# Two transformer blocks on one core: context and x share each weight, modulation sums move to TensorE, attention steps spread by one tile

## What is computed

```python
def first_block(x, c, ...):
    for l in range(2):
        sh1, sc1, gt1, sh2, sc2, gt2 = split(silu(c) @ w_ada[l] + b_ada[l], 6)   # modulation: 1024 -> 6144
        h = rms_norm(x) * (1 + sc1) + sh1
        # h @ w_in, latents, softmax attention and stick-breaking attention, gated merge
        x = x + gt1 * (merged @ w_out[l])
        h = rms_norm(x) * (1 + sc2) + sh2
        x = x + gt2 * ((silu(a) * v) @ w_down[l])       # a, v = split(conv3(h @ w_up[l]))
    return x

def second_block(x, c, ctx, c_ctx, ...):
    for i in range(2):
        mod_x, mod_c = silu(c) @ w_mod[i] + b_mod[i], silu(c_ctx) @ w_mod[i] + b_mod[i]
        hx, hc = rmsnorm(x) * (1 + sc_x) + sh_x, rmsnorm(ctx) * (1 + sc_c) + sh_c
        if i == 0:                     # same weights for hx and hc
            yx, yc = conv_module(hx), conv_module(hc)   # 1024->2048, gate, depthwise conv of 31 taps, layernorm, 1024->1024
        else:                          # keys and values of x and of the context, queries of x
            yx = attention(hx, keys(hx, hc), values(hx, hc))
        x = x + g_x * rmsnorm(yx)      # and ctx likewise while i == 0
        x = x + gf_x * rmsnorm((silu(f @ w1) * (f @ w3)) @ w2)    # and ctx likewise while i == 0
    return x
```

## Time and profile before

| | before |
|---|---|
| median of 3 runs | 3748.67 us (3745.18 to 3753.87) |
| profiled execution | 3750.82 us, its span 3749.0 us, mean granted clock 0.968 |
| busy: PE, DVE, ACT, POOL | 91%, 62%, 38%, 30% |
| HBM read | 368.85 MB, 99 GB/s over the span |
| instructions | 41475 |

### The profile page before, as it was taken

One profiled execution on the slowest core, in us unless ns is written; L12 is line 12 of the kernel. 1 busy time (PEld: TensorE's weight loads), 2 busy tenths in 40 slices (PEclk: granted clock), 3 DMA queues, 4 the chain that ended last, 5 costly groups with the idle time before them and its releaser, 6 DMA issues.

```text
span 3749.0 us, 41475 instructions
## 1 busy us (share of the span) xinstructions
PE 3405.9 (91%) x15776; PEld 2677.8 (71%) x15776; DVE 2312.8 (62%) x3179; ACT 1432.3 (38%) x2194; POOL 1132.4 (30%) x867
## 2 busy tenths in 40 slices
PE   5989999999989998999789997599999977799998
PEld 3757778886658777777659975357888656668886
DVE  6764466564857779496967669944233776643233
ACT  3433233333433233232554454354222455542222
POOL 4404545553404544444411005500000126500000
PEclk8999999999999999999889998799999989999999
DMA  6404535543303434444228721112332100013332
GB/s 207 128 14 124 153 125 159 175 144 90 112 6 121 146 116 122 119 118 138 74 71 241 228 78 45 34 45 85 90 101 79 57 29 1 1 57 96 101 92 66
DMA packets 552730, 373.66 MB, mean 100 GB/s; under 512 B 28861, under 2 KB 526871, under 8 KB 551508
## 3 DMA queue, kind: packets, MB, share of 16 engines
q1 hardware_dynamic: 522928, 278.19, 25.6%
q0 software_dynamic: 29408, 92.76, 7.5%
q10 hardware_dynamic: 196, 0.07, 0.0%
HBM read 368.85 MB, written 2.10 MB: 99 GB/s over the span
## 4 chain that ended last, share of the span: by engine, by line
PE 68%; DVE 24%; issue 3%; ACT 3%; DMA 2%; SPq 0%; POOL 0%; DVEq 0%; ACTq 0%
PE PS L397 18%; PE PS L399 18%; PE PS L398 18%; DVE mod_acc L1086 4%; DVE CV L1232 3%; PE PS L445 3%; DVE tmp L1232 2%; PE PS L468 2%; DVE cv L1575 1%; DVE Wl L1042 1%; PE PS L742 1%; DVE stat_t L1107 1%; PE PS L885 1%; DVE small L1613 1%; PE PS L492 1%
## 5 line engine op out<-in xcount | busy, mean ns | idle before, releaser
L397 PE MATMUL PS<-Hh,Wh 128*128 128x512 f32 (+1 forms) x2816 | 1068.8, 380 | 89.0 <-DVE Wl L1042 62.3
L398 PE MATMUL PS<-Hl,Wh 128*128 128x512 f32 (+1 forms) x2816 | 1045.6, 371 | 0.0
L399 PE MATMUL PS<-Hh,Wl 128*128 128x512 f32 (+1 forms) x2816 | 1045.0, 371 | 0.0
L2100 POOL TENSOR_TENSOR Wl<-raw,Wh 128x1024 fp32r<-128x1024 f32 (+2 forms) x254 | 580.2, 2285 | 711.3 <-ACT Wh L1667 709.4
L397 PEld LDWEIGHTS PS<-Hh,Wh 128*128 128x128 f32 x2816 | 540.5, 192 | 212.1 <-issue 123.8
L1667 ACT ACTIVATE Wh<-raw 128x1024 fp32r<-128x1024 f32 (+2 forms) x558 | 541.2, 971 | 323.8 <-PE PS L399 284.5
L1042 DVE TENSOR_TENSOR Wl<-raw,Wh 128x1024 fp32r<-128x1024 f32 (+2 forms) x304 | 351.0, 1155 | 446.7 <-ACT Wh L1667 446.0
L1086 DVE SCALAR_TENSOR_TENSOR mod_acc<-mod_w,cact,mod_acc 128x256 f32<-128x256 f32 (+1 forms) x644 | 549.5, 895 | 98.7 <-DMA mod_w<-in_w_ada 78.9
L398 PEld LDWEIGHTS PS<-Hl,Wh 128*128 128x128 f32 x2816 | 540.8, 192 | 92.4 <-issue 6.8
L399 PEld LDWEIGHTS PS<-Hh,Wl 128*128 128x128 f32 x2816 | 540.2, 192 | 90.0
L397 PE MATMUL PS<-g_h,Wh 128*128 128x512 f32 (+1 forms) x880 | 337.0, 383 | 14.2 <-DVE g_l L1167 12.5
(11 more groups left out here) (305 smaller groups left out, 4499.5 us busy)
## 6 DMA issues: line engine op xcount, KB each, us to landing
raw<-in_ffn_w SPq DMA_DIRECT2D x132, 512.0 KB, 3.8
mod_w<-in_w_mod POOLq DMA_DIRECT2D x192, 256.0 KB, 3.7
raw<-in_w_up SPq DMA_DIRECT2D x88, 512.0 KB, 4.5
mod_w<-in_w_ada POOLq DMA_DIRECT2D x160, 256.0 KB, 4.0
raw<-in_w_in SPq DMA_DIRECT2D x62, 512.0 KB, 4.2
raw<-in_conv_w_pw SPq DMA_DIRECT2D x48, 512.0 KB, 4.0
raw<-in_ffn_w SPq DMA_DIRECT2D x48, 384.0 KB, 3.3
raw<-in_ffn_w SPq DMA_DIRECT2D x48, 320.0 KB, 3.1
```

The source lines that it names most:

```text
L397: pe.matmul(o, wh, xh, start=start, stop=False, skip_group_check=True)
L398: pe.matmul(o, wh, xl, start=False, stop=False, skip_group_check=True)
L399: return pe.matmul(o, wl, xh, start=False, stop=stop, skip_group_check=True)
L2100: pool.tensor_tensor(low, src, high.bitcast(F32), ALU.subtract).then_inc(*mark("w_low_pool", one[0]))
```

## The change

1. The context is no longer a pass of its own. `conv_both`, `ffn_both` and one `attention_inputs` use every split slab for the 512 columns of x and the 256 of the context (`both`: three matmuls on 512 columns, then three on 256, in two neighbouring PSUM banks). The convolution's buffers hold x, 15 zeros and the context side by side (783 columns), so one instruction does a tap for both; of the taps DVE now has 14, PE 8 and ACT with POOL 9. The feed forward goes in groups of four chunks (`F_GROUPS`). In norms x comes first and then the context, with statistics of its own. The context's input is transposed in the last feed forward of block 1, and x's first squares of block 2 are summed in that feed forward's second half.
2. Modulation: DVE's sums and POOL's loads are gone. SP loads 128x2048 values at a time (1 MB) into one `mod_w`, and a unit on PE (`mod_rows`) is four float32 matmuls of 512 columns with the conditioning vector (one or two columns) as the weights, each to another group of 32 partitions of bank 7. After eight units DVE copies the bank to `mod_row` and PE transposes it (`mod_turn`). There are 8 units in the start-up and 88 in block 1, one after every second slab (every third in the first layer's output product and feed forward).
3. Attention: transposes of tile n-4 instead of n-3 in step n, and the product with the values two steps later.

```diff
-    DVE_TAPS, PE_TAPS = 17, 5
+    SPAN = SEQ + PAD + CTX
+    C_AT = SEQ + PAD
+    DVE_TAPS, PE_TAPS = 14, 8
...
+        def both(job, w, i, cols, x, c, first, last, streams="xc"):
+            b, wh, wl = bank_of[job], w[0][:, i, cols], w[1][:, i, cols]
+            for o, src, one in ((PS[:, b, :], x, "x"), (PS[:, b + 1, 0:CTX], c, "c")):
+                if one in streams:
+                    mm = three(o, wh, wl, src[0], src[1], first, last)
+            return mm
...
+        def mod_rows(block_of, r, w):
+            job, b = ("mod", *block_of), block_of[0]
+            if r == 0:
+                begin(job, "mod")
+            for j in range(4):
+                mm = pe.matmul(PS[32 * j:32 * j + b, bank_of[job], :], cact[b][:, r, :], w[:, 512 * j:512 * (j + 1)],
+                               start=r == 0, stop=r == KD - 1, skip_group_check=True)
+            return mm
+
+        def mod_turn(block_of):
+            job = ("mod_t", *block_of)
+            begin(job)
+            pe.wait_ge(*free(("mod", *block_of)))
+            for q in range(4):
+                mm = pe.transpose(bank(job)[:, q * P:(q + 1) * P], mod_row[:, q * P:(q + 1) * P], const("ident"))
...
-                pe.wait_ge(*ready("mod_w_used", last_tile[g]))
-                for v in range(vs):
-                    for j in range(lo // P, (lo + w) // P):
-                        mm = pe.matmul(bank(job)[:, col:col + 1], acc[n % 2][:, c:c + P], const("ones")[:, 0:1],
+                if what == "rows":
+                    pe.wait_ge(*ready("mod_w_in", block_of, r))
+                    mm = mod_rows(block_of, r, mod_w)
...
+        def ffn_both():
+            for lo, hi in F_GROUPS:
+                for f in range(lo, hi):
...
+                        for x in "13":
+                            linear_both(("up" + x, 0, "x", f), w[x], ("f", 0, "c"))
+                for j in range(KD):
...
+                    for f in range(lo, hi):
+                        mm = both(job, w, f - lo, slice(j % 2 * P, (j % 2 + 1) * P), (g[0][0], g[1][0]), (g[0][1], g[1][1]),
+                                  f == lo, f == hi - 1)
...
-            for n in range(len(tiles) + 5):
+            for n in range(len(tiles) + 7):
                 if n < len(tiles):
                     scores(n, *tiles[n])
-                if n >= 6 and n % 2 == 0:
-                    pv((n - 6) // 2)
-                if 0 <= n - 3 < len(tiles):
-                    turn(n - 3, *tiles[n - 3])
+                if n >= 8 and n % 2 == 0:
+                    pv((n - 8) // 2)
+                if 0 <= n - 4 < len(tiles):
+                    turn(n - 4, *tiles[n - 4])
...
-        load_x("c")
         pre(("n", 0, "c"), CTX)
-        conv_module("c")
-        pre(("f", 0, "c"), CTX)
-        ffn_2(0, "c")
-        pre(("n", 1, "c"), CTX)
-        attention_inputs("c")
-        pre(("n", 0, "x"), SEQ)
-        conv_module("x")
-        pre(("f", 0, "x"), SEQ)
-        ffn_2(0, "x")
-        pre(("n", 1, "x"), SEQ)
-        attention_inputs("x")
+        conv_both()
+        for s in ("x", "c"):
+            pre(("f", 0, s), NS[s])
+        ffn_both()
+        for s in ("x", "c"):
+            pre(("n", 1, s), NS[s])
+        attention_inputs()
...
+            while mod_units and n >= (before[2] + 5 if before else 4):
+                block_of, r, _ = unit = mod_units.pop(0)
+                if before:
+                    sp.wait_ge(*(full(("mod", *before[0])) if before[1] == KD - 1 else ready("mod_w_used", *before[0:2])))
+                sp.dma_start(mod_w[:, :], w_mod.rearrange("(p t) c -> p t c", t=KD)[:, r, :])\
+                  .then_inc(*mark("mod_w_in", block_of, r, by=16))
```

More of the change, by code:

```diff
@@ new lines, in conv_both, with diagonal_taps @@
+                norm_stats(("post", ("conv", "x")), j - 1)
+            norm_stats(("post", ("conv", "x")), KD - 1)
+        def diagonal_taps(j):
+            job = ("taps", j)
+            begin(job, "pair")
+            pe.wait_ge(*free(("pw1a", "x", j)))
+            pe.wait_ge(*ready("diag", j, PE_TAPS - 1))
+            o = banks2(job, SPAN)
+            for at_s in (slice(0, SEQ), slice(C_AT, SPAN)):
+                for k in range(PE_TAPS):
+                    tap = DVE_TAPS + k
+                    mm = pe.matmul(o[:, at_s], diag[:, k, :], U[j % 2][:, at_s.start + tap:at_s.stop + tap],
+                                   start=k == 0, stop=k == PE_TAPS - 1)
@@ L1236, in conv_module @@
                 early_sum = tmp_free[i] = own(dve.tensor_tensor(accs[0], accs[0], accs[1], ALU.add))
+                if j + 1 < KD:
+                    gate(j + 1)
             add_late(KD - 1, early_sum)
-            job = ("mean", s)
-            dve.wait_ge(*full(job))
-            for c in range(KD):
-                ins = dve.scalar_tensor_tensor(CV[:, c, 0:n], bank(job, n), -1.0 / D, CV[:, c, 0:n], ALU.mult, ALU.add)
-                ins.then_inc(*(empty(job) if c == KD - 1 else mark("centred", s, c)))
@@ L1254, in conv_module @@
-            for j in range(KD):
-                ahead(("pw2", s, j))
-            post_norm(("conv", s), n, Y, lambda c: col(2, 0, s, 8, c))
+            where = {"x": slice(0, SEQ), "c": slice(C_AT, SPAN)}
+            for s in ("x", "c"):
+                job, n = ("mean", s), NS[s]
+                dve.wait_ge(*full(job))
+                for c in range(KD):
+                    ins = dve.scalar_tensor_tensor(CV[:, c, where[s]], bank(job, n), -1.0 / D, CV[:, c, where[s]],
+                                                   ALU.mult, ALU.add)
+                    ins.then_inc(*(empty(job) if c == KD - 1 else mark("centred", s, c)))
@@ new lines, in conv_both @@
+                for k in range(PE_TAPS):
+                    act.activation(diag[:, k, :], const("ident"), ACT.Identity,
+                                   scale=vec("w_dw", (DVE_TAPS + k) * KD + j)).then_inc(*mark("diag", j, k))
+                act.wait_ge(*free(("pw1a", "x", j)))
+                if j >= 2:
+                    act.wait_ge(*ready("conv", j - 2))
+                for k in range(-1, LATE_SUMS - 1):
+                    if j + 1 < KD and k in (1, 5):
+                        ahead(("pw1a" if k == 1 else "pw1g", "x", j + 1))
@@ new lines, in conv_both @@
+                    act.activation(o[:, :], U[j % 2][:, tap:tap + SPAN], ACT.Identity, scale=vec("w_dw", tap * KD + j))\
+                       .then_inc(*mark("tap_product", j, k))
+            finish(KD - 1)
+            where = {"x": slice(0, SEQ), "c": slice(C_AT, SPAN)}
+            for s in ("x", "c"):
+                for c in range(KD):
+                    act.wait_ge(*(free(("mean", s)) if c == KD - 1 else ready("centred", s, c)))
+                    square((("ln", s), c), CV[:, c, where[s]], NS[s])
+                root(("ss", ("ln", s)), NS[s])
@@ new lines, in conv_both @@
+            ahead(first_slab(("ln", "x")))
+            act.wait_ge(*full(tally.h_before["ln", "x"]) if tally.h_before.get(("ln", "x")) else full(("pw1g", "x", KD - 1)))
+            for s in ("x", "c"):
+                for c in range(KD):
+                    act.wait_ge(*ready("ln_pre", ("ln", s), c))
+                    o = tb((("ln", s), c))[:, 0:NS[s]]
+                    act.wait_ge(*own(silu(o, o, bias=vec("ln_b", c))))
+                    act.activation(h_of(("ln", s))[0][:, c, :], o, ACT.Copy).then_inc(*mark("h_high", ("ln", s), c))
```

871 lines of the change are left out of this document (463 added, 408 removed).

## The result

| | before | changed |
|---|---|---|
| median, 4 runs each | 3751.27 us | 3641.58 us (3640.9 to 3642.1) |
| ratio | | 0.971 (95% interval 0.969 to 0.973) |
| span of the profiled execution | 3749.0 us | 3639.6 us |

The change made the kernel 2.9% faster. I had forecast faster, but by 0.7% (3723 us). The measured time lies inside the range and nearest to rival A (3609).

A forecast was written before the change was run, and what follows sets the result against it. PE was taken as the main bound, DVE in the convolution's loop, waits in attention. From 3749 us, shared pass -98, modulation on TensorE +114 and attention -42 gave 3723 us, 45 either way; the wider range ran from 3575 to 3835.

The forecast's parts named there:

- rival A: Modulation on PE: all four column groups run at once, 1.06 us a unit, 3609 us in all; chance 0.33.
- T = 5 x 0.43 + 0.20 = 2.35: Cost in us of one modulation unit on PE, partly overlapped; 88 units in block 1 add 207 us.
- The bounds 1.06 and 3.64: Modulation unit's cost in us: all four matmuls overlapping, or none; the latter was a rival at 3837 us, chance 0.18.
- The middle case: Modulation unit: records start in program order, so only neighbouring matmuls overlap; five steps instead of eight, 2.35 us; chance 0.37.
- `vcols` wait: Start-up: a single 17.6 us wait behind the first modulation sums, whose removal was to save 10 us.
- rival C: Modulation loads come late, with one buffer and a place in SP's queue; 0.5 us a unit, 3768 us; chance 0.07.
- 158 GB/s: Load rate needed in block 1 for 1 MB of modulation and two 0.5 MB slabs per unit; expected to fit.
- The shared pass: Context run together with x in convolution, feed forward and keys/values/queries instead of its own pass: -98 us.
- the slope of DVE beside POOL: Convolution's loop: a DVE tap beside a POOL addition costs 3.2 ns more per column, 2.62 us for 783 columns.
- DVE's sums: Block 1, layer 1's feed forward: removing DVE's modulation sums stops delays of weight splits, -43 us, nothing in other slabs.
- Attention: Later transposes and value products loosen a ring of waits between PE, DVE and POOL: -42 us.
- Context matmuls: PE in the shared stages: context matmuls keep their number and cost 0.118 us each behind x's; 1920 add 227 us.

The follow-up runs named there:

- four-group: The changed kernel itself, each modulation unit's four matmuls on four different column groups; 3641.58 us.
- one-group kernel: Changed kernel with all four matmuls of a modulation unit on one column group, another from unit to unit; 3872.5 us.
- kernel with the groups in rows: Changed kernel with a unit's four matmuls on two column groups, in the order first, first, second, second; 3715.0 us.
- start-up kernel: Changed kernel with ACT squaring x ahead of its first weight copies and SP loading positions ahead of the first modulation weights; 3626.1 us.
- kernel with light sums: Kernel before, with DVE's modulation sums after a group's first row cut to 8 columns; 3705.5 us.
- Two kernels: Changed kernel with the old attention steps, 3685.1 us; kernel before with only the new attention steps, 3708.7 us.

## Why the prediction was wrong, and where it was right

**The step that failed** is "T = 5 x 0.43 + 0.20 = 2.35". The bounds 1.06 and 3.64 were right, and measured to 0.03 us by the four-group and the one-group kernel. The middle case took starts in program order, and no row of before spoke for it; the kernel with the groups in rows shows that it isn't so. 88 x 1.29 = 113 us, the whole of rival A. I gave A 0.33 and this 0.37. That the kernel got faster, as forecast, is in part luck: the middle case stood between a bound that makes it faster and one that makes it slower (3609 and 3837), and nothing in the trace of before chose between them.

**With T = 1.06** my own terms give 3610, and 3639.6 was measured. The 30 us in between:
- Start-up. I took -10 for the `vcols` wait. Removing the sums uncovered the next in line, ACT's squares behind loads, and the stretch stayed as long (-0.7). The start-up kernel shows that 15.5 us were there to be had.
- A late load, 9.9 us. This is rival C's mechanism (a load late in SP's queue) at a single place, with another cause than I gave: not the buffer and not the rate, but a wait of SP for PE ahead of another load. Elsewhere in block 1 no unit waited; where I had worked out 158 GB/s, the last feed forward moved 150.
- The shared pass, 9 us short. By stages I had 112, 202 and 30 for convolution, feed forward and keys; measured 117, 198, 38. The chunk was 32.6 us against my 33.1, and the slope of DVE beside POOL predicted 2.62 for 783 columns, measured 2.65. In part that is luck. The time not beside POOL I put at 10.2 us, but my own numbers give (9.4 - 3 x 0.66) x 1.44 = 10.7 before the context's gate, a chunk of 33.6 or more; the measured rest is 32.6 - 22.9 = 9.7. The stage of keys, values and heads is where I was short: its DVE grew from 108 to 132 us, PE's waits for DVE's `stat_v` from 4.7 to 11.0, and PE's own work by 28 (105.3 to 133.4) where the 144 matmuls are 17. No run took that stage apart.
- Some 8 us in block 1. T was read to the product behind; by the 1.18 of the third one, 88 units cost 10 us more. Layer 0's feed forward, where nothing else changed, bears it out: 22 units of 1.18 and 3 turns of 0.6, less 11 groups of one-column records at 0.92 each, give +17.7, and it took 17.5 more. Layer 0's mixer is 4 us over the same sum, and PE's waits in it grew by 4.5 (21.2 to 25.7); why they grew is open.

**DVE's sums** were -43 for the crowded feed forward and nothing elsewhere. The two traces show about -39 there and -7 in layer 1's mixer, and the kernel with light sums 41 and 7.

**Attention** was -42 with POOL and PE next. Two kernels put the step at 43.5 and 44.3, and the trace at 46.

**Context matmuls** at 0.118: the shared feed forward took 574.8 us for x's 1584 and the context's 1584 matmuls; at the two paces these are 356 + 187 = 543, and the rest is its statistics and norms. PE is busy 570 of 575. A stretch of it with nothing but matmuls, as many of x as of the context:

```profile
2400.00:2450.00 50.00, 50.00 (x286) 43.65 (x285) 16.42 (x17) 7.80 (x8) 0.00 (x0) 1.00 0.22 64
```

A pair takes 50/143 = 0.350 us, against 0.225 + 0.118 = 0.343. That sharing saves loads and splits, but not one matmul, held.

## What to carry to other kernels

Matmuls with few columns of weights can be put on separate column groups of TensorE and run side by side; count the records on the busiest group of a unit and price only those, whatever the order, with 0.2 us for going in and out, and read the cost to the third product behind and not to the first. Where an engine is slowed by a neighbour for a fixed time, price an instruction added to it or taken from it at its undisturbed duration, and one added to the neighbour at the slowdown that it brings. Before a wait is booked as saved, look who stands next in that queue: in the start-up the whole saving went to another wait, and reordering the queues gave 15.5 us there and 13.5 at the late load.

## What the runs showed of the hardware that I had not expected

Float32 matmuls (two records each) on different column groups start together whatever their order in the program: eight records take 1.06 us on four groups, 1.91 on two, 3.62 on one. The overlap crosses from one unit to the next, but with one group to a unit only two groups were ever at work: 64 records took 15.6 us (36 steps of 0.43), where no overlap would be 27.5 and four groups at once take 7.0. POOL's subtractions stopped being late when DVE's operations beside them shrank, though POOL's own work stayed the same.
